# Where the kept sum stands at the end of a layer, and what opens the next one: a two-layer hybrid decoder step on one core

## The chip, the core and the metric

One core of one Trainium2 chip runs the whole program. Its engines are TensorE (PE in the profile, its weight loads PEld), VectorE (DVE), ScalarE (ACT), GpSimd (POOL) and SyncE (SP), which here only issues DMAs. The metric is the device time in microseconds, from runs without a profile; a profiled execution gives the trace.

## What is computed

One inference step of two layers over 256 prompt rows and 32 sample rows (8 sequences of 4), width 1024. Each layer is a mixer (three head groups side by side) and a mixture of 32 experts, each followed by a residual sum and a layer norm. What matters here, cut from the reference:

```python
mod = (silu(c) @ w_ada + b_ada)           # six vectors: sh1, sc1, g1, sh2, sc2, g2
h = x * (1.0 + sc1) + sh1
proj = h @ w_in                           # then convolutions, three mixers
mix = concat(y_ssd, y_rg, y_ret) @ w_out
x = layernorm(ALPHA * x + (1.0 + g1) * mix, ln1_g, ln1_b)
h2 = x * (1.0 + sc2) + sh2
moe = _moe(h2, router_w, router_bias)     # top-2 of 32 experts, blocks of rows by expert
x = layernorm(ALPHA * x + (1.0 + g2) * moe, ln2_g, ln2_b)
```

All is 32-bit. The weights pass through the chip once: 2 MB tiles of w_ada, w_in and w_out in the mixer, then 6 MB for each expert block.

## The kernel before

Every engine has its own program, written by hand, and runs it in order; semaphores tie them together. The order of the code is the order of the work. No scheduler moves anything.

**The weight stream.** SP issues all weight loads on one DMA queue. In the mixer it goes through the list STREAM (27 tiles of 2 MB) over three slots of `ring`; a tile is issued when PE has freed its slot (`free_slot`). The list opens with four w_ada tiles (0 to 3) and two w_in tiles. In layer 0, `tokens_in` (L580 to L585: prompt rows, sample rows, router weights, router bias) is issued after the third w_ada tile and ahead of the fourth. For the experts two sets of three slots alternate.

**The head of a layer** (L925 to L985). PE makes the four w_ada products (`ada`, L851 and L854), turns the first two and the last two into columns (`columns`, L902), and turns the prompt rows of x (`turn_x`, L927) between them. After `turn_x` stand three products of a constant whose result nobody reads (`keep_clock(3)`, L909), then `ada(3)`, `columns(1)` and the turning of the 32 sample rows ("xts", L958) into a bank of the rotating plan `bank_plan`. DVE and ACT make h from these banks (`hT`, L2031, L1662, and for the samples L2037 and L2040), and PE's first features (L987) wait for all of it. In layer 1, DVE then multiplies x_tm by ln2_g and adds ln2_b (L2046, six operations), which the residual needs only after the mixer; GpSimd's loads of the late tensors wait for that (`x_whole`). Then come the convolutions, one of 16 tiles after the other (L2074 and L2077), each between PE's feature tile and PE's turning of its result (L1037).

**The end of a layer.** Expert blocks run in pairs. For each block PE makes gate and up (`gate_up`, L1508), ACT the silu, DVE the product and its transpose (`hidden`, L2677 and L2679), and PE the down product (`down`, L1525). The results are spread over the rows with `selw` (L1540) and summed by DVE (`add_up`, L2703 and L2705). The last pair is apart (`last_pair`, L1591). There DVE makes the kept sum, ALPHA * x plus what all earlier pairs gave (`kept`, L2765 to L2773), PE brings it into four banks by a product with the identity (L1606) and adds the last pair's rows to it (L1613). In PE's order the identity products stand behind the second block's gate and up. Between the blocks PE turns the next layer's small vectors (`turn_vectors`, L915 and L918, layer 0 only) and makes five products of a constant (`keep_clock(5, 6)`, L909). DVE's order there is `hidden` of block 0, `weights` (L2690 to L2694), `gated_down` of block 0 (L2753), `take_vectors`, `kept`, `hidden` of block 1, `gated_down` of block 1.

Of the kernel before, what the change touches and what calls it, by code (L numbers as in the profile page):

```python
# [17 lines left out]
P = 128  # L18
# [125 lines left out]
def bank_plan():  # L144


    out = [(("ada", c), "A") for c in range(3)] + [(("mt", 0), "D")] + [(("xt", q), "XY"[q // 2]) for q in range(4)]
    out += [(("ada", 3), "A"), (("mt", 1), "D"), (("xts",), "D")]
    out += [(("rgx", m), "A") for m in range(RT)] + [(("rgg", m), "A") for m in range(RT)]
# [110 lines left out]
def trunk(nc, A, O):  # L260
    cc, _ = const_table()
    ctx = ExitStack()
    with ctx:
# [158 lines left out]
        def C(name, rows=P, lo=0, n=None):  # L422
            a, b = cc[name]
            if b - a == 1 and n is not None:
                return con[0:rows, a:b].to_broadcast([rows, n])
            return con[0:rows, a + lo:(b if n is None else a + lo + n)]
# [5 lines left out]
        def sig(name, per_layer):  # L432
            return Signal(sem(name), per_layer)
# [18 lines left out]
        def emptied(l, key):  # L452

            n = PLACE[key]
            if n >= ROT:
                return takes(l, PLAN[n - ROT][0])
            return (settled, l + 1) if n < 3 or l == 0 else (xhat.sem, xhat.at(l, 0))

        def fills(l, key):

            return filled.at(l, PLACE[key] + 1)

        def bank(key):
            return ps[:, PLACE[key] % ROT, :]
# [53 lines left out]
        var_ready = sig("var_ready", 3 * NT + 2)  # L518
        rstd_ready = sig("rstd_ready", 3 * NT + 2)
        vec_full, vec_taken = sig("vectors_full", 1), sig("vectors_taken", 1)  # L520
        xhat = sig("normed_rows", NT)
# [53 lines left out]
        def _(sp):  # L575
# [13 lines left out]
            for l in range(DEPTH):  # L589
                tb = sp.snap(before)  # L590
                seen = sp.snap(tb + l * STEADY)
                for n, (kind, at) in enumerate(STREAM):
                    s, r = SLOT_OF[n], ROUND_OF[n]
                    if l == 0 and n == NS:
                        tokens_in()
# [225 lines left out]
        def _(pe):  # L821
# [11 lines left out]
            for l in range(DEPTH):  # L833
# [72 lines left out]
                def keep_clock(n_, at=7):  # L906

                    for _ in range(n_):
                        mm(ps[:, at, :], C("ident"), con[:, 0:512], start=True, stop=True)  # L909
# [38 lines left out]
                if l == 0:  # L948
                    pe.wait_ge(vec_taken.sem, vec_taken.at(0, 1))
                keep_clock(3)  # L950
                ada(3, 3)
                free_slot(3)
                columns(1)
                pe.wait_ge(*emptied(l, ("xts",)))
                idle["pe"].stand(pe)
                o = bank(("xts",))
                for k in range(KT):
                    last = tr(o[:, k * TS:(k + 1) * TS], x_tm[0:TS, 2, k * P:(k + 1) * P], C("ident", TS, 0, TS))  # L958
                last.then_inc(FL, 1)
                n = 4  # L960
# [17 lines left out]
                idle["pe"].stand(pe)  # L978
                pe.wait_ge(*takes(l, ("xts",)))
                idle["pe"].stand(pe)  # L980
# [610 lines left out]
                def last_pair(q):  # L1591
# [5 lines left out]
                    if l + 1 < DEPTH:  # L1597
                        turn_vectors(l + 1)
                    keep_clock(5, 6)
                    gate_up(d, 1, 1)  # L1600
                    pe.sem_inc(gt_full, 1)
                    pe.wait_ge(acc_taken, 5 * n_ + 1)
                    pe.wait_ge(kept_sum.sem, kept_sum.at(l, 1))
                    for i in range(2):
                        for a in range(2):
                            mm(ps[:, 4 + 2 * i + a, :], C("ident"), x_tm[:, i, a * 512:(a + 1) * 512], start=True, stop=False,  # L1606
                               skip_group_check=True)
                    down(d, 1)
                    pe.wait_ge(selw_ready, n_ + 1)
# [342 lines left out]
        def _(dve):  # L1952
# [25 lines left out]
            for l in range(DEPTH):  # L1978
# [48 lines left out]
                for q in range(2, 4):  # L2027
# [5 lines left out]
                    last.then_inc(TY, 1)  # L2033
                dve.wait_ge(filled.sem, fills(l, ("xts",)))
                o = bank(("xts",))
                h4s = hT[:, :, SEQ:T].rearrange("p k (b j) -> p k b j", b=DEC_BATCH)
                tt(h4s, o[:, 0:KT * TS].rearrange("p (k b j) -> p k b j", k=KT, b=DEC_BATCH),  # L2037
                   over(modT[:, 1, :, 1:], DEC_SEQ, 3), ALU.mult)
                D()
                tt(h4s, h4s, over(modT[:, 0, :, 1:], DEC_SEQ, 3), ALU.add).then_inc(TD, 1)  # L2040
                if l:
                    dve.wait_ge(ln2_in.sem, ln2_in.at(l - 1, 32))
                    for n_ in range(2):
                        for i in range(NT):
                            x_ = x_tm[0:ROWS[i], i, :]
                            tt(x_, x_, lnp[0:ROWS[i], n_, :], (ALU.mult, ALU.add)[n_])  # L2046
                        D()
                    dve.sem_inc(x_whole.sem, 1)
                dve.wait_ge(lam_ln.sem, lam_ln.at(l, 1))
# [7 lines left out]
                for u in range(RT + XT):  # L2057
# [17 lines left out]
                    for j in range(1, CONV_WIDTH):  # L2075
                        D()
                        stt(c_, r_[:, j:j + CVW], tap(j), c_, ALU.mult, ALU.add)  # L2077
                    dve.drain().then_inc(cv_ready.sem, 1)


# [698 lines left out]
                n_last = dve.snap(spreads + QUADS + rest)  # L2779
                hidden(d, 0)  # L2780
                cpy(scol[2 * BLK:, :], scol[0:2 * BLK, :])
                D()
                weights(P)
                gated_down(d, 0)
                if l + 1 < DEPTH:
                    take_vectors(l + 1)
                kept()
                hidden(d, 1)
# [95 lines left out]
```

## Time and profile before

| what | us |
|---|---|
| three runs without a profile | 1899.48, 1904.38, 1903.30 |
| their median | 1903.3 |
| the profiled execution, its own time | 1896.24 |
| its span, first to last instruction | 1894.3 |
| PE, DVE and ACT busy in the span | 1540.0, 763.9 and 351.4 |
| mean granted TensorE clock | 0.909 of full speed |

The span has six parts in time: the head of layer 0 (to 50.6), its mixer, its experts (from about 477 to 929.9, where the last down product starts), and the same again for layer 1 (features from 964.0, last down product from 1870.9). A row of the timeline reads: start, duration, engine, line, operation, output and inputs, count of instructions merged, and in brackets how long the engine stood idle before it and what released it. PE runs each 32-bit product as two instructions, so five products stand as x10.

### The profile page before, as it was taken

The numbers are of one execution on the slowest core, as the hardware profiler recorded it, in microseconds if no ns is written. First come the engines' busy times: TensorE is split into PE (matmuls) and PEld (weight loads), VectorE is DVE, ScalarE is ACT, GpSimd is POOL, SyncE is SP. The second block draws the span as 40 slices with busy tenths as digits, with TensorE's granted clock in tenths as the row PEclk, the third lists the DMA queues.
The fourth block names the chain that finished last, engine by engine and source line by source line (L and its number), as shares of the span: only waits on it lengthen the run. The fifth ranks groups of instructions, "written<-read, shape, count | busy, mean of one in ns | idle before, by whom it ended". The sixth has DMA issues, their size and how long they took to land.

```text
span 1894.3 us, 29527 instructions
## 1 busy us (share of the span) xinstructions
PE 1540.0 (81%) x11778; PEld 833.7 (44%) x11778; DVE 763.9 (40%) x1694; ACT 351.4 (19%) x777; POOL 136.1 (7%) x170
## 2 busy tenths in 40 slices
PE   5999999997867776677889999998886776677775
PEld 2764543534433343334366555353353343333442
DVE  0353566767312221222535266586742221222226
ACT  1235311221101111010223532120311111011011
POOL 3000013102200000000020000211200000000000
PEclk8999999998988898888989999999988888888888
DMA  9444437537899999999954533745659999999994
GB/s 331 149 178 164 139 99 222 196 115 311 347 407 427 429 427 429 428 429 427 402 201 166 195 123 100 226 134 213 279 245 427 427 428 430 427 430 427 428 429 193
DMA packets 93544, 567.54 MB, mean 300 GB/s; under 512 B 7126, under 2 KB 7998, under 8 KB 68115
## 3 DMA queue, kind: packets, MB, share of 16 engines
q1 hardware_dynamic: 81682, 532.05, 69.1%
q0 software_dynamic: 11776, 34.33, 6.3%
q8 instruction: 57, 0.93, 0.2%
q14 instruction: 29, 0.23, 0.0%
HBM read 550.53 MB, written 15.81 MB: 299 GB/s over the span
## 4 chain that ended last, share of the span: by engine, by line
PE 48%; DMA 40%; DVE 3%; issue 2%; ACT 2%; SPq 1%; PEldq 1%; PEld 1%; DVEq 1%; ACTq 0%
DMA ring<-in_exp_w_up 36%; PE ps L1508 10%; PE ps L1012 9%; PE ps L987 9%; DMA ring<-in_w_ada 3%; PE ps L1369 2%; PE ps L1234 2%; PE ps L851 2%; PE ps L994 2%; PE ps L909 1%; PE ps L1483 1%; DMA ring<-in_w_out 1%; PEldq L891 1%; PE ps L1203 1%; PE ps L1138 1%
## 5 line engine op out<-in xcount | busy, mean ns | idle before, releaser
L1508 PE MATMUL ps<-ring,xTb 128*32 128x256 f32 x4224 | 325.2, 476 | 229.0 <-DMA ring<-in_exp_w_up 223.6
L1508 PEld LDWEIGHTS ps<-ring,xTb 128*32 128x32 f32 x4224 | 162.5, 136 | 391.4 <-issue 346.3
L2677 DVE TENSOR_TENSOR hb<-sg,ps 128x128 f32<-128x128 f32 x66 | 25.0, 379 | 470.0 <-ACT sg L1883 470.0
L1012 PE MATMUL ps<-ring,hT 128*128 128x512 f32 x384 | 171.4, 598 | 0.0
L987 PE MATMUL ps<-hT,ring 128*128 128x288 f32 x640 | 166.0, 419 | 4.8 <-DVE hT L2040 2.5
L1483 PE MATMUL ps<-sel,h_tm 128*128 128x128 f32 (+1 forms) x912 | 163.0, 306 | 0.0
L1483 PEld LDWEIGHTS ps<-sel,h_tm 128*128 128x128 f32 x912 | 124.8, 189 | 53.8 <-issue 25.2
L987 PEld LDWEIGHTS ps<-hT,ring 128*128 128x128 f32 x640 | 123.1, 195 | 43.2 <-issue 8.8
L1883 ACT ACTIVATE sg<-ps 128x128 f32<-128x128 f32 x66 | 18.3, 278 | 591.6 <-PE ps L1508 591.6
L1525 PE MATMUL ps<-ring,hTb 128*32 128x256 f32 x2048 | 123.8, 382 | 2.5 <-DVEq L2680 2.5
L2685 DVE COPY ys<-ps 32x256 f32<-32x256 f32 x124 | 52.6, 424 | 157.4 <-PE ps L1525 156.2
L1012 PEld LDWEIGHTS ps<-ring,hT 128*128 128x128 f32 x384 | 71.0, 190 | 98.8 <-issue 98.3
L1633 ACT ACTIVATE ys<-ps 32x256 f32<-32x256 f32 x140 | 52.3, 374 | 213.8 <-PE ps L1525 212.6
L1540 PE MATMUL ps<-ys,selw 128*128 128x512 f32 x136 | 66.9, 620 | 20.5 <-DVEq L2686 20.5
L1525 PEld LDWEIGHTS ps<-ring,hTb 128*32 128x32 f32 x2048 | 60.0, 109 | 44.9 <-DVEq L2680 3.5
L851 PE MATMUL ps<-ring,cT 128*32 128x512 f32 x384 | 53.6, 663 | 13.7 <-DMA ring<-in_w_ada 13.4
L1234 PE MATMUL ps<-ring,hT 128*128 128x512 f32 x128 | 62.2, 643 | 2.8 <-DVE h_tm L2261 2.8
L2703 DVE TENSOR_TENSOR acc<-acc,ps 128x512 f32<-128x512 f32 x68 | 46.7, 687 | 38.0 <-PE ps L1540 38.0
L2077 DVE SCALAR_TENSOR_TENSOR cv<-raw,vecT,cv 128x312 f32<-128x312 f32 x96 | 52.2, 544 | 7.2
L909 PE MATMUL ps<-con 128*128 128x512 f32 x88 | 49.1, 706 | 3.7 <-ACT hT L1633 3.7
L1540 PEld LDWEIGHTS ps<-ys,selw 128*128 128x128 f32 x136 | 21.6, 188 | 59.9 <-issue 36.8
L1234 PEld LDWEIGHTS ps<-ring,hT 128*128 128x128 f32 x128 | 25.8, 207 | 33.7 <-issue 30.2
(484 smaller groups left out, 1694.4 us busy)
## 6 DMA issues: line engine op xcount, KB each, us to landing
ring<-in_exp_w_gate SPq DMA_DIRECT2D x66, 2048.0 KB, 18.8
ring<-in_exp_w_up SPq DMA_DIRECT2D x66, 2048.0 KB, 23.3
ring<-in_exp_w_down SPq DMA_DIRECT2D x64, 2048.0 KB, 24.7
ring<-in_w_ada SPq DMA_DIRECT2D x24, 2048.0 KB, 10.4
ring<-in_w_in SPq DMA_DIRECT2D x22, 2048.0 KB, 8.7
ring<-in_w_out SPq DMA_DIRECT2D x8, 2048.0 KB, 8.9
h0s<-in_state_ssd POOLq DMA_DIRECT2D x16, 512.0 KB, 7.2
out_ssd_s<-h0s POOLq DMA_DIRECT2D x16, 512.0 KB, 5.3
```

The source lines that it names most:

```text
L851: mm(o[32 * g:32 * g + 32, :], cT[:, k, :], w[:, k, :], start=(r == 0), stop=False, skip_group_check=True)
L909: mm(ps[:, at, :], C("ident"), con[:, 0:512], start=True, stop=True)
L987: last = mm(o[:, 0:T], w[:, k, m * P:(m + 1) * P], hT[:, k, :], start=(k == 0), stop=(k == KT - 1))
L1012: last = mm(o[:, :], hT[:, k, T0[i]:T0[i] + P], w[:, k, :], start=(k == 0), stop=(k == KT - 1))
L1234: last = mm(o[:, :], hT[:, k, T0[i]:T0[i] + P], w[k // 4][:, k % 4, a * 512:(a + 1) * 512], start=(k == 0), stop=(k == KT - 1))
L1483: last = mm(o, h_tm[0:ROWS[i], i, k * P:(k + 1) * P], sel[0:ROWS[i], i, 0:n], start=(i == 0), stop=(i == NT - 1))
L1508: last = mm(ps[32 * j:32 * j + 32, b, 0:2 * P], xTb[:, k, m * BLK:(m + 1) * BLK], w[:, 0:2, k * D_EXPERT + j * P:k * D_EXPERT + (j + 1) * ...
L1525: last = mm(ps[32 * c:32 * c + 32, 2 + b, 0:2 * P], hTb[:, b, j * BLK:(j + 1) * BLK], w[:, j * D_MODEL + c * 256:j * D_MODEL + (c + 1) * 256],
L1540: last = mm(o[:, :], selw[:, T0[i]:T0[i] + P], ys[:, a * 512:(a + 1) * 512], start=True, stop=True)
L1633: cp = lambda o_, i_: f(o_, i_, ACT.Copy)
L2077: stt(c_, r_[:, j:j + CVW], tap(j), c_, ALU.mult, ALU.add)
L2685: cpy(ys[m * BLK:(m + 1) * BLK, c * 256:(c + 1) * 256], ps[32 * c:32 * c + 32, 2 + b, 0:2 * P])
```

## The change

At the end of a layer:
- DVE: `weights` and `kept` now stand ahead of `hidden` of block 0.
- PE: the identity products stand ahead of the second block's `gate_up`. In layer 0 they also wait for `take_vectors` (`vec_taken`), since they overwrite its bank. The constant products between the blocks are three, not five.

In the head of a layer:
- The sample rows are turned right after `turn_x`, into bank 7, with two semaphores of their own (`few_full`, `few_taken`), in the place where three constant products stood; these are gone. "xts" leaves the bank plan, so that all later entries take the bank before theirs.
- In layer 0, `tokens_in` is issued behind the fourth w_ada tile.
- In layer 1, the six operations on x_tm come after the fourth convolution, not before the first.

```diff
-    out += [(("ada", 3), "A"), (("mt", 1), "D"), (("xts",), "D")]
+    out += [(("ada", 3), "A"), (("mt", 1), "D")]
...
-                    if l == 0 and n == NS:
+                    if l == 0 and n == NS + 1:
                         tokens_in()
...
-                keep_clock(3)
+                for k in range(KT):
+                    last = tr(ps[:, 7, k * TS:(k + 1) * TS], x_tm[0:TS, 2, k * P:(k + 1) * P], C("ident", TS, 0, TS))
+                last.then_inc(few_full.sem, 1)
                 ada(3, 3)
...
-                    keep_clock(5, 6)
-                    gate_up(d, 1, 1)
-                    pe.sem_inc(gt_full, 1)
+                    keep_clock(3, 6)
                     pe.wait_ge(acc_taken, 5 * n_ + 1)
+                    idle["pe"].stand(pe)
                     pe.wait_ge(kept_sum.sem, kept_sum.at(l, 1))
+                    idle["pe"].stand(pe)
+                    if l + 1 < DEPTH:
+                        pe.wait_ge(vec_taken.sem, vec_taken.at(l + 1, 1))
+                        idle["pe"].stand(pe)
...
+                    gate_up(d, 1, 1)
+                    pe.sem_inc(gt_full, 1)
                     down(d, 1)
...
+                    if l and u == RT - 1:
+                        dve.wait_ge(ln2_in.sem, ln2_in.at(l - 1, 32))
+                        for n_ in range(2):
+                            for i in range(NT):
+                                x_ = x_tm[0:ROWS[i], i, :]
+                                tt(x_, x_, lnp[0:ROWS[i], n_, :], (ALU.mult, ALU.add)[n_])
+                            D()
+                        dve.sem_inc(x_whole.sem, 1)
...
+                cpy(scol[2 * BLK:, :], scol[0:2 * BLK, :])
+                D()
+                weights(P)
+                kept()
                 hidden(d, 0)
-                cpy(scol[2 * BLK:, :], scol[0:2 * BLK, :])
-                D()
-                weights(P)
                 gated_down(d, 0)
                 if l + 1 < DEPTH:
                     take_vectors(l + 1)
-                kept()
                 hidden(d, 1)
```

DVE's own program at the end of layer 0, from the first instruction behind the loop over the earlier pairs, before (hb and hTb are `hidden`, scol to scol `weights`, ys `gated_down`, vecT and halo `take_vectors`, h_tm<-accs the start of `kept`):

```order
L2677 TENSOR_TENSOR hb<-sg,ps 128x128
L2679 STREAM_TRANSPOSE hTb<-hb 128x128
L2781 COPY scol<-scol 64x1
L2690 SCALAR_TENSOR_TENSOR selw<-dbc,scol 128x288
L2691 SCALAR_TENSOR_TENSOR selt_132<-dbc,scol 128x288
L2693 TENSOR_TENSOR selw<-selw,selt_132 128x288
L2694 TENSOR_SCALAR scol<-scol 128x1
L2751 REGISTER_ALU
L2753 TENSOR_TENSOR ys<-ps,gate 32x256 x4
L1982 COPY vecT<-ps 128x108
L1983 COPY halo<-ps 128x384
L2765 COPY h_tm<-accs 32x256 x4
```

And in the changed kernel, where line numbers are two higher:

```order
L2782 COPY scol<-scol 64x1
L2692 SCALAR_TENSOR_TENSOR selw<-dbc,scol 128x288
L2693 SCALAR_TENSOR_TENSOR selt_132<-dbc,scol 128x288
L2695 TENSOR_TENSOR selw<-selw,selt_132 128x288
L2696 TENSOR_SCALAR scol<-scol 128x1
L2767 COPY h_tm<-accs 32x256 x4
L2769 TENSOR_TENSOR acc<-acc,gate 128x1024 x2
L2771 TENSOR_TENSOR h_tm<-h_tm,gate 32x1024
L2773 SCALAR_TENSOR_TENSOR x_tm<-x_tm,acc 128x1024 x2
L2775 SCALAR_TENSOR_TENSOR x_tm<-x_tm,h_tm 32x1024
L2677 ISA
L2679 TENSOR_TENSOR hb<-sg,ps 128x128
```

All of `weights` and `kept` moved ahead of hb; the vectors and the gated rows stayed behind it.

PE's program at the same place, before (L1508 is `gate_up`, L1525 `down`, L915 and L918 the vectors, L909 the constant products, L1606 the identity products):

```order
L1525 MATMUL ps<-ring,hTb 32x256 x16
L915 MATMUL ps<-con,vrow 128x108
L918 MATMUL ps<-con,hrow 128x24 x16
L909 MATMUL ps<-con 128x512 x5
L1505 REGISTER_ALU
L1508 MATMUL ps<-ring_121,xTb 32x256 x32
L1602 ISA
L1606 MATMUL ps<-x_tm,con 128x512 x4
L1520 REGISTER_ALU
L1525 MATMUL ps<-ring_121,hTb 32x256 x16
```

And changed:

```order
L1522 MATMUL ps<-ring,hTb 32x256 x16
L916 MATMUL ps<-con,vrow 128x108
L919 MATMUL ps<-con,hrow 128x24 x16
L910 MATMUL ps<-con 128x512 x3
L1597 ISA
L1606 MATMUL ps<-x_tm,con 128x512 x4
L1502 REGISTER_ALU
L1505 MATMUL ps<-ring_121,xTb 32x256 x32
L1517 REGISTER_ALU
L1522 MATMUL ps<-ring_121,hTb 32x256 x16
```

The identity products moved ahead of the second `gate_up`, and two constant products went.

SP's program at the start of layer 0, before:

```order
L578 DMA con<-in_con 128x1965
L609 DMA ring<-in_w_ada 128x8x512 x3
L582 DMA x_tm<-in_x_prompt 128x2x1024
L583 DMA x_tm<-in_x_sample 32x1024
L584 DMA rw<-in_router_w 128x256
L585 DMA rbias<-in_router_bias 128x32
L609 DMA ring<-in_w_ada 128x8x512
```

And changed:

```order
L579 DMA con<-in_con 128x1965
L610 DMA ring<-in_w_ada 128x8x512 x4
L583 DMA x_tm<-in_x_prompt 128x2x1024
L584 DMA x_tm<-in_x_sample 32x1024
L585 DMA rw<-in_router_w 128x256
L586 DMA rbias<-in_router_bias 128x32
```

The fourth w_ada tile moved ahead of the four token loads.

## Rows read from the trace of the kernel before

**Rows 1.** Timeline of layer 0's end: start, duration, what, idle before and releaser.
```profile
908.66 3.66 PE L1508 MATMUL ps<-ring,xTb 128*32 128x256 f32 x64 [0.19 <-issue]
908.82 0.42 DVE L2705 TENSOR_TENSOR accs<-accs,ps 128x256 f32<-128x256 f32 x1 [0.19 <-issue]
...
912.70 0.38 DVE L2677 TENSOR_TENSOR hb<-sg,ps 128x128 f32<-128x128 f32 x1 [3.46 <-ACT sg L1883]
...
913.59 1.93 PE L1525 MATMUL ps<-ring,hTb 128*32 128x256 f32 x32 [1.27 <-DVEq L2680]
913.63 0.15 DVE L2781 COPY scol<-scol 64x1 f32<-64x1 f32 x1
...
915.26 0.15 DVE L2694 TENSOR_SCALAR scol<-scol 128x1 f32<-128x1 f32 x1
...
916.80 4.56 PE L909 MATMUL ps<-con 128*128 128x512 f32 x10
...
918.24 1.17 DVE L2765 COPY h_tm<-accs 32x256 f32<-32x256 f32 x4
...
922.66 3.66 PE L1508 MATMUL ps<-ring,xTb 128*32 128x256 f32 x64 [1.30 <-DMA ring<-in_exp_w_up]
...
925.47 1.21 DVE L2773 SCALAR_TENSOR_TENSOR x_tm<-x_tm,h_tm 32x1024 f32<-32x1024 f32 x1
...
929.88 1.93 PE L1525 MATMUL ps<-ring,hTb 128*32 128x256 f32 x32
```

**Rows 2.** Timeline of layer 1's end.
```profile
1850.90 0.42 DVE L2705 TENSOR_TENSOR accs<-accs,ps 128x256 f32<-128x256 f32 x1 [0.19 <-issue]
...
1863.70 3.66 PE L1508 MATMUL ps<-ring,xTb 128*32 128x256 f32 x64 [1.74 <-DMA ring<-in_exp_w_up]
...
1870.92 1.93 PE L1525 MATMUL ps<-ring,hTb 128*32 128x256 f32 x32
```

**Rows 3.** Windows: length, busy us by engine, granted clock, DMA share, GB/s.
```profile
861.00:862.00 1.00, 0.00 (x0) 0.00 (x0) 0.00 (x0) 0.00 (x0) 0.00 (x0) 0.50 1.00 426
892.00:894.00 2.00, 1.85 (x20) 0.96 (x24) 0.00 (x0) 0.00 (x0) 0.00 (x0) 0.50 0.98 414
894.00:895.00 1.00, 1.00 (x18) 0.46 (x13) 0.00 (x0) 0.00 (x0) 0.00 (x0) 0.58 1.12 475
```

**Rows 4.** Timeline of layer 1's head.
```profile
943.69 1.92 PE L851 MATMUL ps<-ring,cT 128*32 128x512 f32 x16 [1.39 <-DMA ring<-in_w_ada]
...
950.43 3.96 PE L909 MATMUL ps<-con 128*128 128x512 f32 x6
...
961.75 1.03 PE L958 MATMUL ps<-con,x_tm 32*128 32x32 f32 x8 [2.28 <-ACT hT L1662]
...
963.66 7.04 DVE L2046 TENSOR_TENSOR x_tm<-x_tm,lnp 128x1024 f32<-128x1024 f32 x6
...
964.04 18.67 PE L987 MATMUL ps<-hT,ring 128*128 128x288 f32 x64 [1.26 <-DVE hT L2040]
```

**Rows 5.** DMA issues in 938 to 941: KB each, us to landing.
```profile
ring<-in_w_ada SPq DMA_DIRECT2D x1, 2048.0 KB, 9.1
```

**Rows 6.** Timeline of layer 0's head.
```profile
22.35 0.62 SPq L585 DMA_DIRECT2D rbias<-in_router_bias  x1
23.08 0.67 SPq L609 DMA_DIRECT2D ring<-in_w_ada  x1
...
34.70 3.59 PE L927 MATMUL ps<-con,x_tm 128*128 128x128 f32 x16
```

**Rows 7.** DMA issues in 22 to 24: KB each, us to landing.
```profile
ring<-in_w_ada SPq DMA_DIRECT2D x1, 2048.0 KB, 16.8
...
rbias<-in_router_bias SPq DMA_DIRECT2D x1, 16.0 KB, 12.3
```

**Rows 8.** Timeline of layer 1's first convolutions.
```profile
1003.07 1.78 DVE L2077 SCALAR_TENSOR_TENSOR cv<-raw,vecT,cv 128x312 f32<-128x312 f32 x3
...
1015.01 0.41 PE L1037 MATMUL ps<-con,xsT 128*128 128x128 f32 x2 [0.26 <-issue]
```

More of the change, by code:

```diff
@@ L519, in trunk @@
         rstd_ready = sig("rstd_ready", 3 * NT + 2)
+        few_full, few_taken = sig("few_rows_turned", 1), sig("few_rows_taken", 1)
         vec_full, vec_taken = sig("vectors_full", 1), sig("vectors_taken", 1)
@@ L953, in _ @@
                 columns(1)
[L954 to L959, printed above, removed]
                 n = 4
@@ L978, in _ @@
                 idle["pe"].stand(pe)
-                pe.wait_ge(*takes(l, ("xts",)))
+                pe.wait_ge(few_taken.sem, few_taken.at(l, 1))
                 idle["pe"].stand(pe)
@@ L2033, in _ @@
                     last.then_inc(TY, 1)
-                dve.wait_ge(filled.sem, fills(l, ("xts",)))
-                o = bank(("xts",))
+                dve.wait_ge(few_full.sem, few_full.at(l, 1))
+                o = ps[:, 7, :]
                 h4s = hT[:, :, SEQ:T].rearrange("p k (b j) -> p k b j", b=DEC_BATCH)
@@ L2039, in _ @@
                 D()
[L2040 to L2046, printed above, removed]
-                        D()
-                    dve.sem_inc(x_whole.sem, 1)
+                tt(h4s, h4s, over(modT[:, 0, :, 1:], DEC_SEQ, 3), ALU.add).then_inc(few_taken.sem, 1)
                 dve.wait_ge(lam_ln.sem, lam_ln.at(l, 1))
@@ L2779, in _ @@
                 n_last = dve.snap(spreads + QUADS + rest)
-                hidden(d, 0)
                 cpy(scol[2 * BLK:, :], scol[0:2 * BLK, :])
@@ L2783, in _ @@
                 weights(P)
+                kept()
+                hidden(d, 0)
                 gated_down(d, 0)
```

## The prediction

> **What bounds the kernel now.** I read the chain of waits first. It runs through the experts by way of DMA, through the mixers and the heads by way of PE. Then I read the timeline at the four places that the change touches. At layer 0's end the second block's gate and up start at 922.66, released by their weights after 1.30 us of idle time; at layer 1's end the same at 1863.70 after 1.74 us [rows 1, 2]. Only what comes after these two points, or what delays PE past them, moves a layer's end. What comes after is: gate and up to 926.32, the identity products until the second down product starts at 929.88, so 3.56 us on the chain [rows 1]. The change aims at these. Ahead of the point PE has slack, and fills part of it with constant products (4.56 us from 916.80) [rows 1]. The heads are chains of PE, DVE and ACT with one DMA wait, 1.39 us for the third w_ada tile [rows 4].
>
> **Layer 0's end.** The change takes the identity products off the part behind the weights, but puts `weights` and `kept` ahead of `hidden` of block 0 on DVE. DVE runs in order. Behind it wait PE's first down product, everything behind that in PE's order, and with it the identity products and the second gate and up. So the question is when `hidden` is done.
>
> DVE ends the last sum of the pair before at 909.24 (908.82 + 0.42). I allow 0.7 us for the end of the loop, so 909.94. `weights` takes 1.8 (913.63 to 915.41). `kept` with its sample part takes 8.44 (918.24 to 926.68). `hidden` until PE can start takes 0.89 (912.70 to 913.59) [rows 1]. Sum: 909.94 + 1.8 + 8.44 + 0.89 = 921.1. Before, the down product started at 913.59. From there PE needs 1.93 for the down product, 1.28 for the vectors (915.52 to 916.80), 2.74 for three constant products (three fifths of 4.56), 3.6 for the identity products, 3.66 for gate and up, and 1.27 until the down product of block 1 (912.32 to 913.59) [rows 1]. That is 14.5, so 935.6 in place of 929.88: **5.7 us later**, though 3.6 us left the old chain. DVE's `take_vectors`, for which PE now waits too, falls under the constant products and costs nothing.
>
> The clock comes on top. PE is now idle from 912.3 to 921.1. In this trace the clock is at half speed (1.2 GHz) at 861 to 862, where PE is idle, and is still there at 892 to 894, in PE's first two microseconds of work after a wait; it rises in 894 to 895 [rows 3]. In the old order PE is idle for only 1.27 and 1.30 us here, and gate and up take the full-speed 3.66 [rows 1]. At half speed the down product costs 1.9 more and the vectors some 0.3. I take 2.2, bounds 0 and 3. So the second down product starts **7.9 us later** (5.7 to 8.7).
>
> The Trainium skill (TensorE: Matmul & The Clock Gate, "Loop structure matters more than you think") says that a long wait between groups of products lets PE go cold. By it the 2.2 us are due; without it the term would be 5.7. This speaks against dropping the fillers while PE gets a longer wait.
>
> **Layer 1's head.** It starts 7.9 late and gives some back. The wait for the third tile (1.39) shrinks to the usual gap: -1.25. The three constant products go: -3.96, and -0.2 for the turned samples that now lie ready when DVE comes to them; their turning moves up: +1.03 [rows 4]. The fourth tile's load is issued 7.9 later, at about 947.8, and took 9.1 to land [rows 5], so 956.9. PE asks for it at about 958 (the constant products ended and `ada(3)` began near 954.3; 954.3 + 7.9 - 1.25 - 3.96 + 1.03 = 958.0). The load is just hidden. Net for the features at 964.04: 7.9 - 1.25 - 3.96 + 1.03 - 0.2 = **+3.5** (1.3 to 5). The features already run their first part slowly (18.67 for 64) [rows 4], and I leave that as it is.
>
> **The residual's rows.** Six operations, 7.04 us, stood in 963.66 to 970.70, while the first feature tile was made: no gain from taking them out [rows 4]. Now they stand behind the fourth convolution, which ends at 1004.85. PE turns the fifth tile at 1015.01 [rows 8]. DVE is then free at about 1012.0, and its next convolution, with its four steps and small copies, takes 2.8 (the spacing when it runs without a wait, which I read as 0.5 + 1.78 [rows 8] and small steps). With an ACT copy of under 1 us between them PE starts at about 1015.8: **+0.8** (0 to 2). Every later tile leaves DVE some slack, so the lag dies out. GpSimd's late loads move back by some 41 us and are needed much later: nothing.
>
> **Layer 0's head.** The token loads now stand behind the fourth w_ada tile. The router bias, the last of the four, was issued at 22.35 and landed after 12.3 us, at 34.65; `turn_x` started at 34.70 [rows 6, 7]. So tokens were what PE waited for. The tile was issued at 23.08 and landed after 16.8 us, at 39.9 [rows 6, 7], so 5.25 for 2 MB. The DMA engines are busy throughout, so the order of issue is the order of landing here, and the tokens swap with the tile: they land at about 39.9, PE idles from 34.6 to there. From the start of `turn_x` to the fourth product was 34.70 to about 40.8 = 6.1 before; now it is 3.59 [rows 6] + 1.03. The head changes by 5.25 - 6.1 + 4.6 = +3.8 less 0.2 for the samples, plus about 0.9 for a fourth product partly at half speed after the idle time: **+4.5** (-1.8 to +6). The lower bound is no delay of the tokens at all.
>
> **Layer 1's end.** As layer 0's, without the vectors (-1.28). DVE stands 1.04 later against the weights (1850.90 - 908.82 = 942.08, where the weights and the down product are 941.04 apart) [rows 1, 2]. So 5.7 - 1.3 + 1.0 = 5.4 at full speed; the down product and part of the fillers at half speed add 2: **+7.4** (5.4 to 8.3). Nothing behind it gives anything back, it is the end of the program.
>
> **The sum.** 4.5 + 3.5 + 0.8 + 7.4 = 16.2 us. Against the profiled execution's own 1896.24 that gives 1912.4. The median of the runs is 1903.3, 7.1 higher than this one execution; the runs spread over 4.9. I add the sum to the median: **1919.5**. The ends of the terms add to +4.9 and +21.3.
>
> **Rivals.**
> 1. PE stays at full speed in all new gaps, or is back at once. For it: between 912.3 and 913.6 it stayed. Against: [rows 3]. Without the clock terms (2.2 + 2 + 0.9): 1914.4.
> 2. The tokens are not held up behind the tile. DMA engines run apart from each other, and small loads could pass. Then the head of layer 0 gains 6.1 - 4.6 + 0.2 = 1.7 and the sum is 10.0: 1913.3. Against: the landings came in the order of issue. The Trainium skill (DMA: Bandwidth & Descriptors, "Queues, rings and completion order") says that completion is not first in, first out per issuing engine; by that this rival would be possible.
> 3. Both at once, and the head of layer 1 takes in most of the first delay: -1.7 + 1.3 + 0.3 + 5.4 = 5.3: 1908.6, within 0.3%.
> 4. Faster. The identity products leave the part behind the weights and nothing else is late: -3.56 at each end, -1.7 in layer 0's head, -3 in layer 1's: 1891.5. It holds if `hidden` is ready by 922.66 - (3.6 + 2.74 + 1.28 + 1.93) = 913.1 in layer 0. By the rows DVE would need to do 11.1 us of work in 3.2. It would need the kept sum to be much shorter than measured. Against: nothing in it changes size.
>
> **How the numbers follow.** Forecast 0.64, rival 1 0.12, rival 2 0.10, rival 3 0.09, rival 4 0.05. The forecast's own range is 1915 to 1925; with rivals 1 and 2 and the bounds of the clock it becomes 1910 to 1925. A measurement of this kernel can tell 0.3%, 5.7 us, from no change. Slower by more: 0.86; within: 0.09; faster: 0.05.
>
> **What would show it.** In the new trace: at each layer's end DVE's six operations of `kept` ahead of hb, PE idle for about 9 us ahead of the first down product, and gate and up of block 1 released by PE's own order instead of a DMA. If the second gate and up still wait for their weights, the main term is wrong. In layer 0's head: `turn_x` at about 40 with PE idle before it; if it still starts near 34.7, rival 2 is right. In layer 1's head: no DMA wait at the third tile, and features about 3.5 later against the first expert of layer 0 than before. At the fifth convolution of layer 1: a PE wait of up to 1 us. The forecast falls if DVE's loop end or PE's order hides the kept sum, which nothing in the rows allows.

## The result, and the profile after

The changed kernel took **1922.46 us** (median of 4 runs, 1917.53 to 1925.93) beside 1902.09 for the kernel before on the same chip: a ratio of **1.0106, 95% interval 1.0075 to 1.0136**. On another chip it gave 1.0087 (1.0052 to 1.0123, 5 runs, below). So it is slower by more than 0.3%, and the 1919.5 forecast lies 3 us below the median. The profiled execution has a span of 1923.1 us, 28.8 longer than the span of before; 12 of these are absent from a second profile of the same kernel. The profiled execution of before lies at the low end of its runs (1896.24 us beside the median of 1902.09), so the medians, 20.4 us apart, are the better measure of the loss.

I cut both spans at the same products: the first features of a layer, the first gate and up of its experts, the first gate and up of its last pair, the second down product of its last pair. The right-hand column is a second profile of the same changed kernel, from a later set of runs.

| stretch, us | before | after | difference | after, second profile |
|---|---|---|---|---|
| layer 0's head | 50.58 | 56.99 | +6.41 | 53.28 |
| its mixer | 426.27 | 427.63 | +1.36 | 426.31 |
| its experts | 431.81 | 437.47 | +5.66 | 433.49 |
| layer 0's end | 21.22 | 30.88 | +9.66 | 27.98 |
| layer 1's head | 34.16 | 31.01 | -3.15 | 31.01 |
| its mixer | 427.61 | 428.90 | +1.29 | 428.86 |
| its experts | 458.95 | 459.05 | +0.10 | 459.15 |
| layer 1's end | 20.32 | 27.75 | +7.43 | 27.74 |
| rest | 23.38 | 23.42 | +0.04 | 23.38 |
| span | 1894.30 | 1923.10 | +28.80 | 1911.20 |

Layer 0's end in the timeline of the changed kernel (start, duration, what, idle time before and what ended it), to hold beside [rows 1]:

```profile
922.09 3.66 PE L1505 MATMUL ps<-ring,xTb 128*32 128x256 f32 x64
...
925.14 1.17 DVE L2767 COPY h_tm<-accs 32x256 f32<-32x256 f32 x4
...
932.36 1.21 DVE L2775 SCALAR_TENSOR_TENSOR x_tm<-x_tm,h_tm 32x1024 f32<-32x1024 f32 x1
933.50 0.36 DVE L2679 TENSOR_TENSOR hb<-sg,ps 128x128 f32<-128x128 f32 x1
...
934.38 3.64 PE L1522 MATMUL ps<-ring,hTb 128*32 128x256 f32 x32 [8.62 <-DVEq L2682]
...
940.15 4.53 PE L910 MATMUL ps<-con 128*128 128x512 f32 x6
...
944.51 3.60 PE L1606 MATMUL ps<-x_tm,con 128*128 128x512 f32 x8
948.04 3.66 PE L1505 MATMUL ps<-ring,xTb 128*32 128x256 f32 x64
...
952.97 1.93 PE L1522 MATMUL ps<-ring,hTb 128*32 128x256 f32 x32 [1.27 <-DVEq L2682]
```

PE stands still for 8.62 us ahead of the first down product, where before it was 1.27: DVE makes the whole kept sum (925.14 to 933.5) before hb. The second gate and up, which waited for its weights before, now follows the identity products without a gap. The windows of the same place (length, busy us of PE, weight loads, DVE, ACT, GpSimd, granted clock, DMA share, GB/s):

```profile
922.00:930.00 8.00, 3.75 (x68) 2.06 (x64) 7.11 (x15) 0.28 (x1) 0.00 (x0) 1.00 1.01 426
930.00:943.00 13.00, 8.62 (x53) 4.65 (x54) 6.47 (x11) 1.50 (x4) 0.00 (x0) 0.50 1.02 386
...
945.00:950.00 5.00, 5.00 (x44) 2.28 (x46) 0.00 (x0) 0.00 (x0) 0.00 (x0) 1.00 0.78 292
950.00:964.00 14.00, 11.38 (x109) 4.22 (x105) 8.26 (x17) 3.56 (x8) 0.00 (x0) 1.00 0.01 2
```

From 930 to 943 PE has 1.2 GHz (0.50), and the down product takes 3.64 in place of 1.93, the three constant products (two records each, hence x6) 4.53. From 950 to 964 the DMA engines are nearly idle (0.01), where in the kernel before they are at 0.96 to 1.05 from 925 to 944: what had been issued has landed, SP issues the next tile only when PE has freed its slot, and PE is still catching up.

Layer 1's end, beside [rows 2]:

```profile
1871.93 3.66 PE L1505 MATMUL ps<-ring,xTb 128*32 128x256 f32 x64
...
1884.49 3.64 PE L1522 MATMUL ps<-ring,hTb 128*32 128x256 f32 x32 [8.90 <-DVEq L2682]
1888.06 3.33 PE L910 MATMUL ps<-con 128*128 128x512 f32 x6
...
1899.68 1.93 PE L1522 MATMUL ps<-ring,hTb 128*32 128x256 f32 x32 [1.27 <-DVEq L2682]
```

Layer 1's head, beside [rows 4]. The wait of 1.39 for the third w_ada tile is gone; `columns` and `turn_x` follow:

```profile
965.68 1.92 PE L852 MATMUL ps<-ring,cT 128*32 128x512 f32 x16 [0.29 <-issue]
...
968.77 1.92 PE L903 MATMUL ps<-con,qkvg 128*128 128x9 f32 x16 [0.82 <-ACT qkvg L1635]
970.55 3.36 PE L928 MATMUL ps<-con,x_tm 128*128 128x128 f32 x16
```

Layer 0's head, beside [rows 6]:

```profile
40.24 3.65 PE L928 MATMUL ps<-con,x_tm 128*128 128x128 f32 x16 [5.18 <-issue]
...
44.81 3.64 PE L852 MATMUL ps<-ring,cT 128*32 128x512 f32 x16
...
49.99 3.56 PE L903 MATMUL ps<-con,qkvg 128*128 128x9 f32 x16 [0.96 <-ACT qkvg L1635]
...
56.99 3.70 PE L984 MATMUL ps<-hT,ring 128*128 128x288 f32 x7 [3.44 <-DVE hT L2042]
```

The tokens swapped places with the fourth tile. Beside [rows 7], the DMA issues of the changed kernel in 19 to 29 (KB each, us to landing). The tile is issued at 19.30 and lands at 35.6; the router bias is issued at 28.23 and lands at 40.1, and `turn_x` starts at 40.24:

```profile
ring<-in_w_ada SPq DMA_DIRECT2D x1, 2048.0 KB, 16.3
...
rbias<-in_router_bias SPq DMA_DIRECT2D x1, 16.0 KB, 11.9
```

The residual's rows, beside [rows 8]: the six operations on x_tm push the fifth convolution, and PE waits 0.72 for ACT's copy behind it.

```profile
1023.95 7.04 DVE L2078 TENSOR_TENSOR x_tm<-x_tm,lnp 128x1024 f32<-128x1024 f32 x6
...
1034.55 0.44 PE L1034 MATMUL ps<-con,xsT 128*128 128x128 f32 x2 [0.72 <-ACT xsT L1694]
```

### The profile page after: what moved, and what is told of

Read it like the earlier page. It is cut to its first block, busy times and chain, and to the rows that moved or that the text cites. A ratio compares the mean times of both kernels' runs of the same rounds, so it can differ in the third digit from the quotient of the medians.

```text
span 1923.1 us, 29488 instructions
## 1 busy us (share of the span) xinstructions
PE 1549.6 (81%) x11758; PEld 837.0 (44%) x11758; DVE 763.5 (40%) x1694; ACT 350.8 (18%) x777; POOL 135.7 (7%) x170
## 4 chain that ended last, share of the span: by engine, by line
PE 48%; DMA 37%; DVE 6%; issue 3%; ACT 2%; DVEq 2%; PEldq 1%; SPq 1%; PEld 1%; ACTq 0%
DMA ring<-in_exp_w_up 34%; PE ps L1505 9%; PE ps L1009 8%; PE ps L984 8%; PE ps L1366 2%; PE ps L1231 2%; PE ps L852 2%; PE ps L991 2%; DMA ring<-in_w_ada 2%; PE ps L1480 2%; PE ps L910 1%; PE ps L1522 1%; DMA ring<-in_w_out 1%; PE ps L1200 1%; PEldq L892 1%
## 5 line engine op out<-in xcount | busy, mean ns | idle before, releaser
L1522 PE MATMUL ps<-ring,hTb 128*32 128x256 f32 x2048 | 130.1, 397 | 20.1 <-DVEq L2682 20.1
L852 PE MATMUL ps<-ring,cT 128*32 128x512 f32 x384 | 56.1, 692 | 12.8 <-DMA ring<-in_w_ada 12.2
L910 PE MATMUL ps<-con 128*128 128x512 f32 x68 | 41.5, 761 | 3.7 <-ACT hT L1635 3.7
```

The costliest lines, as they stand in the source:

```text
L852: mm(o[32 * g:32 * g + 32, :], cT[:, k, :], w[:, k, :], start=(r == 0), stop=False, skip_group_check=True)
L1522: last = mm(ps[32 * c:32 * c + 32, 2 + b, 0:2 * P], hTb[:, b, j * BLK:(j + 1) * BLK], w[:, j * D_MODEL + c * 256:j * D_MODEL + (c + 1) * 256],
```

## The experiments

The kernels of e1 to e4 ran on one chip, those of e5 to e8 on a second, those of e9 to e11 on a third, each set beside 19 to 27 runs of the kernel before, whose medians were 1902.86, 1902.61 and 1902.63 us. A ratio is always against these; it is given as recorded with its 95% interval, and the quotient of two medians differs from it by up to 0.12%.

**e1: both layer ends as changed, all else as before.** In DVE's code (PE's order at the ends is changed with it, as in the diff above):

```diff
-                hidden(d, 0)
                 cpy(scol[2 * BLK:, :], scol[0:2 * BLK, :])
                 D()
                 weights(P)
+                kept()
+                hidden(d, 0)
                 gated_down(d, 0)
                 if l + 1 < DEPTH:
                     take_vectors(l + 1)
-                kept()
                 hidden(d, 1)
```

> Kernel before with only the two layer ends changed (VectorE makes the weights and the kept sum ahead of the first block's hidden product; TensorE's identity products ahead of the second gate and up, three constant products between). Theory, VectorE's order holds the first down product back: each end takes 7.4 to 9.7 us longer from the last pair's first gate and up to its second down product, layer 1's head gives 1.3 back at the third tile's wait, so +14 us (12 to 17) against before. Rival, the token loads and the heads make most of the loss: under +6 us here. Rival, the clock makes it: PE at full speed everywhere in the last pair would leave +10.

1919.37 us (7 runs), ratio 1.0075 (1.0042 to 1.0108), so +14.3 us by the ratio and +16.5 by the medians. The stretches of the two ends are 27.97 and 28.30, where before has 21.22 and 20.32: +6.75, a little under what I had expected for an end, and +7.98. The ends alone account for most of the loss.

**e2: the tokens' loads behind the fourth tile, all else as before.**

```diff
-                    if l == 0 and n == NS:
+                    if l == 0 and n == NS + 1:
```

> Kernel before with only the token loads issued behind the fourth w_ada tile. Theory, loads land in the order of issue and the tokens swap with a 2 MB tile: the turning of x starts at about 40 in place of 34.7, and nothing is taken in behind it, so +5.3 us (4 to 7). Rival, the tokens are not what is waited for: 0.

1905.74 us (10 runs), ratio 1.0006 (0.9977 to 1.0034): not told from nothing, and less than expected (the medians are 2.9 us apart; the 5.3 us that I had expected, 0.28%, are still inside the interval). The profile suggests why:

```profile
31.21 3.64 PE L851 MATMUL ps<-ring,cT 128*32 128x512 f32 x16
...
35.87 3.55 PE L902 MATMUL ps<-con,qkvg 128*128 128x9 f32 x16 [0.44 <-issue]
40.09 3.33 PE L927 MATMUL ps<-con,x_tm 128*128 128x128 f32 x16 [0.66 <-issue]
```

The tokens did land some 5 us later (the router bias at 40.0; 34.65 before). But in this execution the third w_ada product and the columns ran at 1.2 GHz, at 3.64 and 3.55 us instead of 1.92 each, so PE itself came to `turn_x` only at 39.43 and waited 0.66. In e1, e6, e7 and e10, where the tokens are loaded early, PE starts `turn_x` at 39.03 to 39.75, and there too the third product took 3.64 and the columns 3.56; in the kernel before, in e3 and in e9 both took 1.92 and `turn_x` starts at 34.7 to 35.4. So which of the two happens goes with the granted clock of the execution. PE's wait ahead of `turn_x` with late tokens is 0.66 here, 5.18 and 3.26 in the two profiles of the changed kernel, and 0.73 to 2.94 in e4, e5 and e8: one profile does not price this edit.

**e3: the change with the tokens early again.**

```diff
-                    if l == 0 and n == NS + 1:
+                    if l == 0 and n == NS:
```

> Changed kernel with the token loads back ahead of the fourth tile. Theory: the turning of x starts at 34.7 again, the fourth product waits for its tile until 39.9 at most (the sample rows and no fill end at about 39.3), so 5 to 6.5 us less than the changed kernel and +14 against before. Rival, loss by the dropped constant products: the head stays 2 or more us late, so +17.

1917.05 us (6 runs), ratio 1.0076 (1.0044 to 1.0108), as expected against before. Against the changed kernel it is 0.1% to 0.3% less, where I had expected 5 to 6.5 us, and there is no gain of the new heads over e1 to be seen. `turn_x` starts at 35.38, but the head still takes 52.66, 2.1 more than before. Windows of e3:

```profile
36.00:45.00 9.00, 7.70 (x45) 3.81 (x42) 0.00 (x0) 0.26 (x1) 0.00 (x0) 0.50 1.05 386
45.00:56.00 11.00, 6.90 (x23) 6.00 (x24) 3.48 (x11) 5.25 (x9) 0.00 (x0) 0.50 0.94 346
```

The fourth product and its columns ran at half speed throughout, though PE was busy for 7.70 of 9 us from 36 to 45.

**e4: the change with hb ahead of the weights and the kept sum on DVE.**

```diff
+                hidden(d, 0)
                 cpy(scol[2 * BLK:, :], scol[0:2 * BLK, :])
                 D()
                 weights(P)
                 kept()
-                hidden(d, 0)
```

> Changed kernel with one thing undone: the first block's hidden product is back ahead of the weights and the kept sum on VectorE; the identity products stay ahead of the second gate and up. Theory: the first down product is back at 1.3 us after its gate and up; the kept sum is ready about 10.4 us after the gate and up ends, so the identity products end some 3.6 us after the weights have landed, and each end is 1 to 3 us longer than before, not 8 to 10. In all +6 us against before (4 to 9), most of it the token loads. Rival, what costs is the identity products' new place and the wait for the vectors, not hidden: still +14 or more.

1913.66 us (10 runs), ratio 1.0051 (1.0029 to 1.0072), 10.8 us over before where I had expected 6. The first down product comes at once, 1.26 us behind gate and up. Then PE stops elsewhere, since its identity products wait for `take_vectors`, which stands behind the kept sum and the gated rows:

```profile
921.96 1.93 PE L1522 MATMUL ps<-ring,hTb 128*32 128x256 f32 x32 [1.26 <-DVEq L2682]
...
935.10 5.36 PE L1606 MATMUL ps<-x_tm,con 128*128 128x512 f32 x8 [7.09 <-DVE halo L1985]
940.39 3.66 PE L1505 MATMUL ps<-ring,xTb 128*32 128x256 f32 x64
```

The wait moved one group of products down and took the slow clock with it (5.36 in place of 3.60; granted clock 0.65 from 935 to 940). Not all of the 7.09 is due to `take_vectors`: PE was done with the constants at 928.0, and the kept sum that the identity products read ended only at 931.0. At layer 1's end, which has no `take_vectors`, the stretch is 24.37 all the same, 4.05 over before. Order alone, with the kept sum in one piece, does not give the first `hidden` and the identity products both.

**e5: the change with PE kept at work ahead of the first down product.** Nine products of a constant, whose result nobody reads, ahead of the first down product at both layer ends:

```diff
                     gate_up(d, 0, 0)
+                    keep_clock(9, 6)
                     down(d, 0)
```

> Changed kernel with nine more constant products ahead of the first down product of the last pair, so that TensorE isn't idle while VectorE makes the kept sum (they take 8.2 us at full speed, the wait is 8.5 us). Theory, half of what the ends lost beyond VectorE's own order is the clock: the granted clock stays at 1.00 there, the first down product takes 1.93 and not 3.64, and from the last pair's first gate and up to its second down product it is 26.5 in layer 0 (30.9 in the changed kernel) and 25.5 in layer 1 (27.8): 4 to 6 us less in all. Rival, the clock falls by chance of the run: same as the changed kernel.

1910.64 us (10 runs), ratio 1.0044 (1.0022 to 1.0066).

```profile
917.65 7.99 PE L910 MATMUL ps<-con 128*128 128x512 f32 x18
926.22 1.93 PE L1522 MATMUL ps<-ring,hTb 128*32 128x256 f32 x32 [0.58 <-DVEq L2683]
...
929.43 2.84 PE L910 MATMUL ps<-con 128*128 128x512 f32 x6
```

DVE ends no sooner, yet the down product has its full-speed 1.93 and the constants 2.84. The stretches are 26.50 and 25.56, as expected: beside before, +5.28 and +5.24. This is the net price of the new order at full clock (granted clock 1.00 from 917 to 945), the shorter part behind the weights already set against it. What the changed kernel pays above that, 4.38 and 2.19 (30.88 and 27.75), is the clock. The whole kernel gained more than I had expected: 0.44% over before against 1.06% and 0.87% is 8 to 12 us, where these stretches account for 3.7 to 6.6. The intervals overlap in part, and where the rest comes from is open.

**e6: the kept sum in parts, in the kernel before.** In DVE's code `kept` is cut in three: the gating of acc (2.36 us) ahead of hb, the sum into x_tm (2.36) behind it, the sample rows after the gated rows. The identity products stand ahead of the second gate and up, as in the change, with two constant products in layer 0 and three in layer 1 in place of five.

```diff
+                kept_gate()
                 hidden(d, 0)
+                kept_main()
+                if l + 1 < DEPTH:
+                    take_vectors(l + 1)
                 cpy(scol[2 * BLK:, :], scol[0:2 * BLK, :])
                 D()
                 weights(P)
                 gated_down(d, 0)
-                if l + 1 < DEPTH:
-                    take_vectors(l + 1)
-                kept()
+                kept_few()
                 hidden(d, 1)
```

> Kernel before with its own heads, and layer ends in which VectorE's kept sum is parted: the product with the gate (2.4 us) ahead of the first hidden product, in VectorE's idle 3.4 us, the sum right behind it, then vectors, weights, gated rows and the sample part; the identity products ahead of the second gate and up, two constant products in layer 0 and three in layer 1. Theory: the kept sum is ready 2.4 us after hidden, all of TensorE's work ends by the time the weights land, and each end is 2 to 3.6 us shorter than before: -5 us (-7 to -3), 18.5 and 17 for the two ends. Rival, the identity products' new place costs in itself (the wait for the vectors, the slow clock): 0 or slower.

**1897.15 us** (12 runs), ratio 0.9972 (0.9956 to 0.9988), as expected. The stretches are 18.41, as expected, and 18.61, where I had expected 17.

**e7: the same layer ends in the changed kernel, tokens early.** Beside e6's edit, in the changed kernel:

```diff
-                    if l == 0 and n == NS + 1:
+                    if l == 0 and n == NS:
...
-                    keep_clock(3, 6)
+                    keep_clock(2 if l + 1 < DEPTH else 3, 6)
```

> The same parted ends with the changed kernel's heads (sample rows turned sooner, no constant products, residual's rows later) but the token loads ahead of the fourth tile. Theory, the heads without constant products run slow: layer 0's head is 2 us longer than before (52.7), layer 1's 1 to 3 us shorter, so within 2 us of the parted ends with the old heads. Rival, the dropped products are a plain gain of 3 to 4 us in each head: 5 or more us faster than those.

**1893.25 us** (10 runs), ratio 0.9950 (0.9931 to 0.9969), faster than both kernels. It is 3.9 us below e6 by the medians, which lies between my theory (within 2) and its rival (5 or more), and the intervals of the two ratios overlap. The stretches are 18.41 and 17.92. Its timeline at layer 0's end:

```profile
909.33 2.36 DVE L2767 TENSOR_TENSOR acc<-acc,gate 128x1024 f32<-128x1024 f32 x2 [0.30 <-issue]
912.34 0.38 DVE L2679 TENSOR_TENSOR hb<-sg,ps 128x128 f32<-128x128 f32 x1 [0.64 <-ACT sg L1885]
...
913.23 1.93 PE L1522 MATMUL ps<-ring,hTb 128*32 128x256 f32 x32 [1.26 <-DVEq L2682]
913.27 2.36 DVE L2773 SCALAR_TENSOR_TENSOR x_tm<-x_tm,acc 128x1024 f32<-128x1024 f32 x2
...
918.25 3.60 PE L1606 MATMUL ps<-x_tm,con 128*128 128x512 f32 x8
921.78 3.66 PE L1505 MATMUL ps<-ring,xTb 128*32 128x256 f32 x64
```

The gating fits into the time in which DVE waits for ACT's silu anyway ([3.46 <-ACT sg] in [rows 1]; 0.64 of it is left), and the sum into the time of the down product and the vectors. The identity products start without a wait. This is what the change set out to do, and it is worth 2.81 us at layer 0's end and 2.4 at layer 1's. At layer 0 part of it is lost again in this profile, since PE reaches the third w_ada tile sooner and waits for it, 3.26 where it was 1.39 [rows 4]:

```profile
942.38 1.92 PE L852 MATMUL ps<-ring,cT 128*32 128x512 f32 x16 [3.26 <-DMA ring<-in_w_ada]
```

**e8: the change with the scaling of x_tm where it was** (ahead of all convolutions).

```diff
+                if l:
+                    dve.wait_ge(ln2_in.sem, ln2_in.at(l - 1, 32))
...
-                    if l and u == RT - 1:
-                        dve.wait_ge(ln2_in.sem, ln2_in.at(l - 1, 32))
```

> Changed kernel with the six operations on the residual's rows back ahead of the first convolution. Theory: no wait of TensorE at the fifth convolution's tile, and 35.16 from the second feature group to the first tile behind it in layer 1, as before (35.74 in the changed kernel): -0.6 us. Rival: their old place held the head back, +1 or more.

1916.74 us, one run, so that the time tells nothing about 0.6 us; the trace does. The fifth tile is ready when PE comes to it, and from the start of the last 64 feature products ahead of it to the next feature tile are 19.14 us, as before; 19.63 in the changed kernel, 19.73 in e5.

```profile
1026.29 0.41 PE L1034 MATMUL ps<-con,xsT 128*128 128x128 f32 x2 [0.26 <-issue]
```

**e9: the change's heads alone**, with the residual's rows late, tokens early and both ends as before. Against the kernel before, in PE's code (DVE's code is changed with it, as in the diff above):

```diff
-                keep_clock(3)
+                for k in range(KT):
+                    last = tr(ps[:, 7, k * TS:(k + 1) * TS], x_tm[0:TS, 2, k * P:(k + 1) * P], C("ident", TS, 0, TS))
+                last.then_inc(few_full.sem, 1)
```

> The kernel before with the change's heads alone: the three constant products behind turn_x gone, the sample rows turned at once, the residual's rows later; the tokens are loaded before the fourth w_ada tile and both layer ends are as before. My theory: each head loses 3.96 of constant products and gets 1 to 2 back as products at half speed, the residual's rows cost 0.6, so the kernel is 2 to 6 us faster than before. Rival, that the slow products eat up all that the constants gave: within 1 us of before or slower. Stretches: layer 0's head about 52 against 50.58 to 55.2 of kernels with the old head, layer 1's about 32.

1899.4 us (10 runs), ratio 0.9974 (0.9952 to 0.9995). The part of the change that drops work is a small gain, inside the 2 to 6 us that I had expected. From `turn_x` to the features are 13.76 us in layer 0 (15.88 before) and 11.84 in layer 1 (15.86). The two heads as wholes were not as expected: layer 0's is 48.48 and not 52, layer 1's is 35.45 and not 32, where two w_ada products ran at half speed (3.64 each) ahead of `turn_x`.

**e10: e7 with the scaling of x_tm back as well** (e8's edit).

> The parted kept sum with the new heads and early tokens, and the scaling of x_tm back where the kernel before has it. If the 0.6 us that PE waits at the fifth tile of layer 1's mixer is all that the moved rows cost, this is 0.6 us faster than the same kernel with the rows late (0.995 of the kernel before), so 0.9945 to 0.995. The stretch from the last group of 64 feature products in front of the first turned tile to the next feature tile: 19.14, not 19.73.

1893.91 us (9 runs), ratio 0.9950 (0.9930 to 0.9969). The stretch around the fifth tile is 19.17, where e7 has 19.72, so the moved rows cost 0.55 us there. In the whole time 0.6 us are below what the measurement tells.

**e11: the changed kernel once more**, with no edit.

> The changed kernel once more, on the chip of the two above, so that the parts and the whole are read against one another. 1.010 of the kernel before again (1.007 to 1.014). If heads and ends add up, the ratio less the ends' part (1.0075) and the tokens' part (up to 1.003) should leave what the heads give; if the heads alone are at 0.998 and the sum is nevertheless 1.010, the parts do not add and the waits behind one another must be looked at.

1917.54 us (5 runs), ratio 1.0087 (1.0052 to 1.0123). Its profile is the last column of the table. In its timeline of layer 0's end the same wait stands, and the clock is back sooner:

```profile
925.23 3.42 PE L1522 MATMUL ps<-ring,hTb 128*32 128x256 f32 x32 [8.50 <-DVEq L2682]
...
929.92 2.84 PE L910 MATMUL ps<-con 128*128 128x512 f32 x6
```

The ratios in a table, by ends and heads:

| | heads as before | heads as changed, tokens early |
|---|---|---|
| ends as before | 1 | 0.9974 (e9) |
| ends as changed | 1.0075 (e1) | 1.0076 (e3) |
| kept sum in parts | 0.9972 (e6) | 0.9950 (e7) |

The ends as changed cost 0.75% to 1.0%, the parted ones give 0.24% to 0.28%. The heads give 0.22% and 0.26% in two rows and nothing in the middle one; with intervals of about 0.3% on each of e1 and e3, that is no proof that the parts fail to add. The three parts alone, ends (e1), heads (e9) and late tokens (e2), add to 0.55%, where the whole measured 0.87% and 1.06%. The intervals are wide enough to allow that too, but whether the parts add stays open.

## Why the prediction was right, step by step

**DVE's order (5.7 of 16.2 at layer 0, 5.4 at layer 1).** Right, and shown: hb waits for the kept sum, PE for hb. The net price is 5.28 and 5.24 us (e5), and hb comes as late as the sum said. My sum allowed 0.7 us for the end of the loop; it was 0.29 (922.95 to 923.24). That undoing the order by itself would give the time back is refuted by e4: the kept sum in one piece is then late itself, and `take_vectors` stands behind it in the same queue. The prediction's note that the latter "costs nothing" holds only while it comes before the identity products are due.

**The clock at the ends (2.2 and 2).** That it falls, as [rows 3] let expect, is shown by e5, which keeps the clock at 1.00 and leaves DVE as late as it was. Its size is 2.19 at layer 1. At layer 0 it is 4.38 in one profile (above my bound of 3) and 1.48 in the other (27.98 - 26.50), because the three constant products take 4.53 us in one and 2.84 in the other, the down product 3.64 and 3.42. The term mis-sized is the stretch at half speed: I took only the down product and the vectors, and the products behind them can run slowly too. Where the clock comes back at layer 0 differs between executions. Both terms of an end together were 7.9 at layer 0, where the two profiles have 9.66 (above the bound of 8.7) and 6.76, and 7.4 at layer 1, where they have 7.43 and 7.42.

**Layer 1's head (-4.4).** It gave back 3.15. The missing part is in two rows: `turn_x` ran partly at half speed (3.36 for 2.46 before; 3.29 for 2.25 to the next start, so 1.04), which I left as it was; and with the DMA wait gone `columns` waits 0.82 for ACT's copy and not 0.44. Against these 1.4 us the samples that lay ready gave 0.37 and not 0.2 (PE's wait for h is 4.20, where the two waits and the turning before took 4.57). The fourth tile's load, priced by [rows 5], was hidden, as computed. The sign that I had named, features about 3.5 us later against the first expert of layer 0 (1.3 to 5), failed in both profiles: 12.2 and 5.3. Of these, 5.66 and 1.68 lie in the experts, which the edit does not touch; the end and the head alone give 6.5 and 3.6.

**The residual's rows (+0.8).** 0.49 to 0.59 (19.14 against 19.63 and 19.73), with a PE wait of 0.72: right. The layer 1 mixer is 1.3 longer in the changed kernel, and 1.55 shorter than before in e7, which has the late rows as well; so the other 0.7 comes from elsewhere. Over all profiles it takes 425.2 to 429.0 us. One place that varies is a group of 14 products behind a wait for ACT, 3.54 us in the changed kernel, 2.93 before and 2.30 in e7; it does not add up to the whole difference, and the rest is open.

**Layer 0's head (+4.5).** The mechanism is right: order of issue was order of landing, `turn_x` at 40.24 where I said 39.9. Rival 2 is out. The size was not: +6.41 in one profile and +2.70 in the other. In the first, the fourth product and its columns ran at half speed to the end (3.64 and 3.56); in the second at full speed (12.87 us from `turn_x` to the features, against 16.75). And the base was a lucky one: in four of the seven profiles with early tokens PE itself is not at `turn_x` before 39, and then late tokens cost what e2 shows, a wait of 0.66 and not of 5. Over the runs the tokens cost little: 0.06% in e2, and 0.1% to 0.3% between e3 and the changed kernel, neither clear of the intervals. So +4.5, a price taken from one profile, is the term that the runs bear out least: it stands for some 1 to 6 us.

**The sum.** 16.2 against the table's 28.8 and 16.9 in two profiles, and 20.4 and 14.9 by the medians. Adding it to the median and not to the one profiled execution was the better choice: 1912.4 would have been 10 too low. That the total came within 3 us is partly luck: the +4.5 of layer 0's head was priced against one execution with a short head, layer 1's head gave back less than the sum said, and layer 0's experts and end vary by several us between executions. The three parts measured alone (0.55%, 10.5 us) would have put the kernel at about 1913. Of the first profile's 28.8, 5.66 lie in layer 0's experts, which the change does not touch. There one gate and up ran slowly, and the products after it too:

```profile
900.04 6.59 PE L1505 MATMUL ps<-ring,xTb 128*32 128x256 f32 x64 [3.28 <-DMA ring<-in_exp_w_up]
906.56 4.57 PE L1480 MATMUL ps<-sel,h_tm 128*128 128x64 f32 x24
...
911.06 3.64 PE L1522 MATMUL ps<-ring,hTb 128*32 128x256 f32 x32
...
915.90 5.71 PE L1537 MATMUL ps<-ys,selw 128*128 128x512 f32 x8 [1.20 <-DVEq L2688]
```

In the kernel before the same gate and up took 4.96. That stretch takes 431.5 to 437.5 us over all my profiles, with 437.5 in the changed kernel, in e4 and in e6, the last of which is faster than before. It varies with the execution, not with the edit. Layer 1's experts, 458.7 to 464.6 us, vary as well.

**The rivals.** Rival 1 (the clock stays) is refuted by both ends; rival 2 by the landing, and rival 3, which needs both, with them; rival 4 (faster) failed where I put its condition, at hb by 913.1. In e7 the down product that waits for hb starts at 913.23, PE makes two constant products in place of three, and the second gate and up starts at 921.78, without a wait. The condition was the right one, and cutting the kept sum in parts all but meets it; "nothing in it changes size" overlooked that the kept sum can be cut.

## What to carry to other kernels

An operation moved ahead in one in-order queue delays everything behind it there, so the question is not whether its result is wanted sooner but what stands behind it and who waits for that; if only part of it fits into an idle piece of the queue, cut it there. Products that only fill time are not all alike: the heads without theirs were a small gain (e9, 0.26%), while nine of them put into a wait of 8 us gave back 0.4% to 0.6% (e5). Price the clock not for the first product behind a wait but for all up to where a row shows it back. And before adding a wait to a head, look at more than one profile: here one and the same head had lengths 3.7 us apart.

## What the runs showed of the hardware that I had not expected

- The same program has stretches of different lengths on the same data, with the granted clock rising sooner or later. Layer 0's head was 56.99 and 53.28 us in two profiles of the changed kernel. In the kernel before, e1 and e6, which have the same program up to there, `turn_x` started at 34.70, 39.34 and 39.03. The spans of the two profiles of the changed kernel differ by 12 us.
- A working PE stayed at 1.2 GHz through much of a head: in e3 from 36 to 56, in e1 from 24 to 39 (0.50 in the windows), while the kernel before has 2.4 GHz from 29 to 34 and from 39 to 44 with the same products. Why these differ I did not take apart.
- Loads of 16 KB to 2 MB from one queue landed in the order of their issue in both kernels, with the 16 engines full (DMA share 1.05 from 24 to 44 in both): 34.65 and 39.9 before, the swapped order after (35.6 for the tile, 40.1 for the router bias).
